# Attention stage of a hybrid decoder block: each projection in two halves of k, with one score unit and one head's maxima behind each half

## What is computed

```python
z = h @ w_in
q_b = apply_rope(aqkv[:, :, 0], cos, sin)
k_b = apply_rope(aqkv[:, :, 1], cos, sin)
for g, (window, dilation) in enumerate(((128, 1), (512, 4), (2048, 16))):
    s = jnp.where(valid, q @ k.T * 64 ** -0.5, -jnp.inf)   # blockwise, in the order of the dilation
    m = jnp.max(s, axis=-1)
    p = jnp.exp(s - m[..., None])
    l = jnp.sum(p, axis=-1)
    o = p @ v
wts = jnp.exp(ms - jnp.max(ms, axis=0))
o_b = (sum(wts * o) / sum(wts * l)) * silu(ag)
```

## Time and profile before

| | us |
|---|---|
| median of 3 runs | 1558.94 |
| lowest, highest | 1557.24, 1559.28 |
| profiled execution, its own time | 1559.48 |
| its span | 1557.7 |
| PE busy | 1536.4 |
| DVE busy | 835.1 |
| ACT busy | 671.9 |

### The profile page before, as it was taken

How to read it: one execution, slowest core, us unless ns; L and a number is a source line. 1 busy time by engine, 2 the same in 40 slices (tenths; PEclk the granted TensorE clock), 3 DMA queues, 4 the chain that set the end, 5 groups by cost and what they waited for, 6 DMA issues and landing times.

```text
span 1557.7 us, 21170 instructions
## 1 busy us (share of the span) xinstructions
PE 1536.4 (99%) x8088; PEld 1298.3 (83%) x8088; DVE 835.1 (54%) x1372; ACT 671.9 (43%) x842; POOL 46.8 (3%) x40
## 2 busy tenths in 40 slices
PE   7999999999999999999999999999999999999998
PEld 6888888888888888888888888888888888788987
DVE  6646565564636463767832574257435654643523
ACT  6646565555656474634323324332423235311211
POOL 2000000000000000002000000000000000000000
PEclk9999999999999999999999999999999999999999
DMA  5121211111111112122312121222122223232611
GB/s 213 42 68 55 68 47 47 54 67 54 67 54 54 54 54 67 54 81 68 95 42 55 55 69 56 56 55 60 50 56 67 55 89 109 95 128 96 243 42 81
DMA packets 33892, 113.73 MB, mean 73 GB/s; under 512 B 5338, under 2 KB 5788, under 8 KB 33820
## 3 DMA queue, kind: packets, MB, share of 16 engines
q1 hardware_dynamic: 33828, 112.82, 22.5%
HBM read 81.77 MB, written 18.45 MB: 64 GB/s over the span
## 4 chain that ended last, share of the span: by engine, by line
PE 97%; DVE 1%; DMA 1%; ACT 0%; SPq 0%; issue 0%
PE z_ps L629 21%; PE z_ps L627 21%; PE z_ps L628 21%; PE pc L792 4%; PE pb L654 3%; PE z_ps L857 2%; PE z_ps L859 2%; PE z_ps L858 2%; PE pa L738 1%; PE pb L775 1%; PE pb L760 1%; PE pb L771 1%; PE pb L768 1%; PE pc L691 1%; PE pb L646 1%; PE pa L859 1%
## 5 line engine op out<-in xcount | busy, mean ns | idle before, releaser
L627 PE MATMUL z_ps<-h_hi,w_hi 128*128 128x512 f32 x1392 | 557.2, 400 | 0.0
L629 PE MATMUL z_ps<-h_hi,w_lo 128*128 128x512 f32 x1392 | 549.5, 395 | 0.0
L628 PE MATMUL z_ps<-h_lo,w_hi 128*128 128x512 f32 x1392 | 549.1, 394 | 0.0
L629 PEld LDWEIGHTS z_ps<-h_hi,w_lo 128*128 128x128 f32 x1392 | 261.8, 188 | 61.4
L627 PEld LDWEIGHTS z_ps<-h_hi,w_hi 128*128 128x128 f32 x1392 | 262.3, 188 | 56.8 <-issue 0.4
L628 PEld LDWEIGHTS z_ps<-h_lo,w_hi 128*128 128x128 f32 x1392 | 262.3, 188 | 56.4
L1216 DVE TENSOR_TENSOR w_lo<-w_stage,w_hi 128x1024 fp32r<-128x1024 f32 x89 | 110.1, 1237 | 260.0 <-ACT w_hi L957 259.6
L965 ACT ACTIVATE zz<-z_ps 128x512 f32<-128x512 f32 x48 | 28.7, 598 | 213.4 <-PE z_ps L629 139.1
L965 ACT ACT_TABLE_LOAD x61 | 78.3, 1283 | 77.4 <-PE z_ps L629 76.7
L957 ACT ACTIVATE w_hi<-w_stage 128x1024 fp32r<-128x1024 f32 x89 | 93.8, 1054 | 0.4
L792 PE MATMUL pc<-pt,vb 128*128 128x128 f32 x560 | 76.9, 278 | 0.7 <-ACT pt L1123 0.7
(11 more groups left out here) (250 smaller groups left out, 2257.3 us busy)
## 6 DMA issues: line engine op xcount, KB each, us to landing
w_stage<-w_in SPq DMA_DIRECT2D x88, 512.0 KB, 3.5
z_swap<-zz SPq DMA_DIRECT2D x96, 128.0 KB, 2.3
gate_d<-gate SPq DMA_DIRECT2D x16, 512.0 KB, 3.7
x_in<-x SPq DMA_DIRECT2D x8, 512.0 KB, 7.4
o_a_d<-o_a SPq DMA_DIRECT2D x8, 512.0 KB, 4.7
w_stage<-w_a SPq DMA_DIRECT2D x8, 512.0 KB, 3.3
cos_t<-gate_d SPq DMA_DIRECT2D x8, 512.0 KB, 3.3
sin_t<-gate_d SPq DMA_DIRECT2D x8, 512.0 KB, 4.0
```

The lines of the kernel that those rows point to most:

```text
L627: nc.tensor.matmul(z_ps[hf][:], w_hi[s][:, k, :], h_hi[:, k, t], start=k == 0, stop=False)
L628: nc.tensor.matmul(z_ps[hf][:], w_hi[s][:, k, :], h_lo[:, k, t], start=False, stop=False)
L629: last = nc.tensor.matmul(z_ps[hf][:], w_lo[s][:, k, :], h_hi[:, k, t], start=False, stop=k == KT - 1)
```

## The change

PE's projection of a slot is cut in two: the first four steps of k (`front`), and the last four (`back`), into the same PSUM bank. Where there are units or maxima, all units of the slot but the last and the maxima of the first half of the list (head 0; in slot 16 the first pair (g, m)) stand between front and back; the last unit and the other maxima stand behind back. ACT's exponentials of the units that went between the halves now stand before the `take` of the slot. Nothing is added or removed, and DVE, POOL and SP have the program they had. Iteration 4 is as before.

```diff
--- before.py
+++ after.py
@@ -617,17 +617,21 @@
                         x_transpose(KT * hf + k + 4)
                 last.then_inc(z_made[hf], 1)
 
-            def project(n, s, hf):
-
-                if hf == 0:
-                    pe.wait_ge(w_lo_done, n + 1)
-                pe.wait_ge(z_taken[hf], n)
+            front, back = range(0, KT // 2), range(KT // 2, KT)
+
+            def project(n, s, hf, ks=range(KT)):
+
+                if ks[0] == 0:
+                    if hf == 0:
+                        pe.wait_ge(w_lo_done, n + 1)
+                    pe.wait_ge(z_taken[hf], n)
                 t = slice(HALF * hf, HALF * (hf + 1))
-                for k in range(KT):
+                for k in ks:
                     nc.tensor.matmul(z_ps[hf][:], w_hi[s][:, k, :], h_hi[:, k, t], start=k == 0, stop=False)
                     nc.tensor.matmul(z_ps[hf][:], w_hi[s][:, k, :], h_lo[:, k, t], start=False, stop=False)
                     last = nc.tensor.matmul(z_ps[hf][:], w_lo[s][:, k, :], h_hi[:, k, t], start=False, stop=k == KT - 1)
-                last.then_inc(z_made[hf], 1)
+                if ks[-1] == KT - 1:
+                    last.then_inc(z_made[hf], 1)
 
             def level_product(i, j):
 
@@ -796,17 +800,28 @@
             def attention(i, prev, cur):
                 for slot in range(2 * AT_CHUNKS):
                     c = slot // 2
+                    units = UNIT_SLOTS.get(slot, ()) if prev else ()
+                    peaks = [(g, m, h) for g, m in MAX_SLOTS.get(slot, ()) for h in range(2)] if cur else []
+
+                    def unit(u):
+                        scores_t(i, u)
+                        if u:
+                            weighted(i, u - 1)
+
                     if cur:
-                        project(N_HG + i * AT_CHUNKS + c, c % 2, slot % 2)
+                        project(N_HG + i * AT_CHUNKS + c, c % 2, slot % 2, front)
+                        for u in units[:-1]:
+                            unit(u)
+                        for g, m, h in peaks[:len(peaks) // 2]:
+                            maxima(i, g, m, h)
+                        project(N_HG + i * AT_CHUNKS + c, c % 2, slot % 2, back)
                     if first(i):
                         hgrn_tail(HEADS, slot)
                         if slot == 6:
                             pe.wait_ge(on_done, HEADS)
                     if prev:
-                        for u in UNIT_SLOTS.get(slot, ()):
-                            scores_t(i, u)
-                            if u:
-                                weighted(i, u - 1)
+                        for u in units[-1:] if cur else units:
+                            unit(u)
                         if slot == 11:
                             weighted(i, N_UNITS - 1)
                     if not cur:
@@ -818,10 +833,8 @@
                                 branch(0, 0, hf, (4, 5, 6, 7))
                             elif slot == 13:
                                 branch(0, 1, hf, (0, 1, 2))
-                    if cur:
-                        for g, m in MAX_SLOTS.get(slot, ()):
-                            for h in range(2):
-                                maxima(i, g, m, h)
+                    for g, m, h in peaks[len(peaks) // 2:]:
+                        maxima(i, g, m, h)
                     if cur and slot == 17:
                         maxed, summed = value(pe, i * N_MAX + N_MAX), value(pe, i * N_SUMS)
                         pe.wait_ge(const_in, 32)
@@ -1084,7 +1097,18 @@
                         for b in range(2):
                             dst = vb[:, g, 4 * b:4 * b + 4, :].rearrange("p c (x e) -> p c x e", e=EDIM)[:, :, 0:3:2, :]
                             nc.scalar.activation(dst, pb[:, b, :].rearrange("p (c x e) -> p c x e", c=4, x=2), ACT.Copy).then_inc(av_taken, 1)
+                    units = UNIT_SLOTS.get(slot, ()) if prev else ()
+
+                    def weigh(u):
+                        act.wait_ge(st_made, (i - 1) * N_UNITS + u + 1)
+                        cols = sum(P * k for _, _, k in unit_keys(UNITS[u][0], UNITS[u][2]))
+                        if u >= 2:
+                            act.wait_ge(pu_made, (i - 1) * N_UNITS + u - 1)
+                        nc.scalar.activation(pt[u % 2][:, 0:cols], pb[:, u % 2, 0:cols], ACT.Exp).then_inc(pt_done, 1)
+
                     if cur:
+                        for u in units[:-1]:
+                            weigh(u)
                         if c < 6:
                             if not first(i) or c >= 2:
                                 act.wait_ge(rope_sum, i * 6 + c - 1)
@@ -1114,13 +1138,8 @@
                         nc.scalar.activation(r_den[EDIM:P, :], acc[1][0:EDIM, :], ACT.Ln).then_inc(den_ln, 1)
                         act.wait_ge(den_ln, 2 * i)
                         nc.scalar.activation(r_den[:], r_den[:], ACT.Exp, scale=-1.0).then_inc(den_done, 1)
-                    if prev:
-                        for u in UNIT_SLOTS.get(slot, ()):
-                            act.wait_ge(st_made, (i - 1) * N_UNITS + u + 1)
-                            cols = sum(P * k for _, _, k in unit_keys(UNITS[u][0], UNITS[u][2]))
-                            if u >= 2:
-                                act.wait_ge(pu_made, (i - 1) * N_UNITS + u - 1)
-                            nc.scalar.activation(pt[u % 2][:, 0:cols], pb[:, u % 2, 0:cols], ACT.Exp).then_inc(pt_done, 1)
+                    for u in units[-1:] if cur else units:
+                        weigh(u)
                     if not cur:
 
                         if 1 <= slot < N_BR:
```

## The result

The changed kernel takes 1562.56 us, the median of 8 runs (1561.04 to 1563.59); the kernel before, in 8 runs beside it, 1558.79 (1557.24 to 1560.36). The ratio is 1.0026, 95% interval 1.0016 to 1.0035: a small slowdown, 3.8 us, clear of the noise. The profiled execution takes 1563.13 us, its span is 1561.4 us.

The account below looks back on a forecast made before the run. PE, busy throughout the attention stage, was taken as the bound. Boundaries 0.7, iteration 0's waits 1.74 and slot 15's 1.6 sum to 4.1 us, against the median 1558.94 giving 1563.0; range 1559.3 to 1566.5.

Parts of the forecast that it names:

- What bounds the kernel: Attention stage: PE busy 601.74 of 601.74 us, so no PE wait is left for the change to take away.
- rival of hidden waits: Weighted matmuls, slots 3 to 10 of iterations 1 to 3: hidden 0.1 us waits go, -4.1 us, 1554.8; chance 0.03.
- Part 1, boundaries: Projection cuts, iterations 0 to 3: 54 more excursions at 0.013 us each, 0.7 us in all.
- Part 2, exponentials: ACT's exponentials ahead of the take cost nothing; without cover each of the 27 slots with a front unit would pay.
- Part 3, iteration 0: PE waits for DVE's row maxima in slots 9, 11 and 13: 0.86, 0.18 and 0.70 us, delay 1.74.
- rival of absorbed waits: Iteration 0: DVE's work moves ahead, waits absent or absorbed; +0.7 to +2.3 us, about 1560.4; chance 0.29.
- Part 3, slot 15: Slot 15, four iterations: PE waits 0.41 us each for row maxima, whose release comes 0.24 later; 1.6 us.
- Slot 13 of iterations 1 to 3: Row maxima released at 1082.33, asked for at 1082.45: just passes without a wait, margin 0.12 us.
- The lengths of the iterations: Profile after: iteration 0 longer by about 2.3 to 2.4 us, iterations 1 to 3 by about 0.6 each.
- The lock: Iteration 0: DVE's chain slips with PE, so waits add up, +4.3 for 1.74; +6.7, 1565.6; chance 0.06.
- The clock: PE's granted clock falls behind the new waits, all seven adding 10 us: 1566 to 1573; chance 0.04.

Follow-up runs that it names:

- maxima undivided: Changed kernel with both heads' maxima behind the back half again, cut and units between the halves kept; ratio to before 0.9997.
- 24 further ones: Changed kernel with 24 more excursions out of the projection in slots 3 to 10 of iterations 1 to 3; ratio to before 1.0020.
- later cut: Changed kernel with its projection cut behind step 6 of 8 instead of 4; ratio to before 0.9999.
- short product: Changed kernel with DVE's product of z_swap and the sines done for 64 of 1024 columns in iteration 0; ratio to before 1.0005.
- second bank: Changed kernel with the maxima of slots 9, 11 and 13 of iteration 0 written to PSUM pair pb; ratio to before 1.0006.
- undivided slot 13: Changed kernel, but in slot 13 alone both heads' maxima stand behind the whole projection; ratio to before 1.0011.
- cut behind step 2: Changed kernel with its projection cut behind step 2 instead of 4; 1574.57 us against 1559.38 before, ratio 1.0097.
- exponentials behind the take: Changed kernel with ACT's exponentials of the front units back behind the take in slots 3 to 10; 1571.31 us, ratio to before 1.0079.

## Why the prediction was right

Its number was 1563.0; measured is 1562.56, and +3.8 against the forecast +4.1. The stage, which is what the sum describes, lost 3.3; that the medians stand nearer to the forecast than the stage does is chance within their noise (the interval is 2.5 to 5.5 us). The stage makes up the 3.3 from 1.66 in slots 9, 11 and 13, 1.25 in the four slots 15 and 0.4 elsewhere; the prediction had 1.74, 1.64 and 0.7. By its own steps:

- **What bounds the kernel.** Right: PE had no wait that the change could take away. The rival of hidden waits would have shown shorter slots with units; slots 3 to 10 of iteration 1 are 0.01 to 0.03 longer. With all maxima undivided, the units between the halves gave back nothing.
- **Part 1, boundaries.** Predicted 0.7 us, 0.013 for each of 54. Measured, beside slot 15, iterations 1 to 3 lost 0.12 to 0.17 each, 0.44 in 45 excursions, 0.01 each; 24 further ones took nothing. The range (0 to 0.02) held. The Trainium skill ("TensorE: Matmul & The Clock Gate", Part 2, "Step-by-step") has only an isolated matmul pay its drain; by that page's warm formula 54 excursions isolated twice would be an estimated 18 us, near 1577. No run shows a boundary that isolates a matmul.
- **Part 2, exponentials.** Right that they cost nothing in the new order, and that, for one, slot 3 pays 0.64 us without it. The cover is less even than the text had it: the shortfall without the edit falls on 18 slots, not on every slot with a front unit.
- **Part 3, iteration 0.** Slot 9: 0.86 predicted, 0.80 measured. Slot 11: 0.18 and 0.21. Slot 13: 0.70 and 0.65. The later cut, the short product and the second bank each take these away by another road: asked later, released sooner, not needed. The rival of absorbed waits needed DVE to gain 0.86 us by slot 9; it gained 0.02.
- **Part 3, slot 15.** 0.41 predicted each time; 0.29 to 0.32 measured. The path was right, as the undivided slot 13 shows, but two terms were mis-sized. The request was put 2.79 us behind the slot's start, half of what slot 9's projection takes. Slot 15 starts behind transposes, and there the first step takes 0.31 us instead of 0.23. The kernel before, iteration 2, the second and the thirteenth matmul of slot 15 (the first is in the earlier trace rows):

```profile
1092.85 0.39 PE L628 MATMUL z_ps<-h_lo,w_hi 128*128 128x512 f32 x1
...
1095.40 0.40 PE L627 MATMUL z_ps<-h_hi,w_hi 128*128 128x512 f32 x1
```

The half is 1095.40 - 1092.54 = 2.86 us there, so PE asks 0.07 later than the sum has it. The other term is the lag: put at 0.20, it is 0.06 from DVE's end to PE's start and 0.10 of slower restart, 0.16. With both the sum gives 0.41 - 0.07 - 0.04 = 0.30.
- **Slot 13 of iterations 1 to 3** just passed, as said (6.03 or 6.04 us against 6.05 or 6.06 before).
- **The lengths of the iterations** grew by less than forecast, for the same terms: iteration 0 by 1.95 us instead of 2.3 to 2.4, iterations 1 to 3 by 0.44 to 0.47 each instead of about 0.6.
- **The lock** did not come: slots 10 and 12 took 6.05 and 6.06 (6.07 and 6.03 before), and the cut behind step 2 made iteration 0 longer by 5.1 and not 9. **The clock** did not fall in the stage, with waits of up to 0.7 us and, with the earlier cut, sixteen shown waits of up to 1.5: the granted clock is 1.00 over the stage in both.

## What to carry to other kernels

Where an engine is never idle, as PE in this stage, moving its own work ahead has no wait to remove, but it asks for its inputs earlier. So list for each moved instruction when its release comes, and which engine sets it. Count how late that release is against the schedule of before: each earlier wait has already made the request later and covers a part of it. Measure the distance from a slot's start to the request in the very slot, since not every half projection takes the same. And see what stands behind the moved work: here the projection's end came later by one head's maxima, and a chain over ACT and DVE charged that to PE two slots further on.

## What was not expected of the hardware

PE has one longer wait that has nothing to do with the change, near 1360 us: it waits for DVE, and DVE for a load of the gates. What the clock does behind it differs from run to run. The changed kernel, PE's waiting instruction and the window behind it; then the kernel with slot 13 undivided:

```profile
1362.90 0.47 PE L870 MATMUL z_ps<-h_hi,w_hi 128*128 128x512 f32 x1 [2.03 <-DVE part L1602]
...
1363.30:1366.30 3.00, 3.00 (x9) 2.35 (x8) 1.50 (x4) 0.00 (x0) 0.00 (x0) 0.50 0.42 168
```

```profile
1360.81 0.47 PE L870 MATMUL z_ps<-h_hi,w_hi 128*128 128x512 f32 x1 [2.30 <-DVE part L1602]
...
1360.80:1363.80 3.00, 2.99 (x13) 2.47 (x14) 1.77 (x4) 0.00 (x0) 0.00 (x0) 1.00 0.53 214
```

After 2.03 us of waiting the clock stood at 0.50, 1.2 GHz, for the next 3 us; after 2.30 us in the other it stayed at 1.00. Of eleven profiles six have the fall (before, changed, maxima undivided, both other cuts, exponentials behind the take) with 278.2 to 278.5 us from the last slot of iteration 3 to the end, and five don't, with 276.3 to 277.1. The length of the wait does not sort them: 1.97 to 2.31 us in the six, 1.78 to 2.30 in the five. The mean granted clock of the whole run does: 0.998 in the six, 0.999 or 1.000 in the five. By the same mark 27 runs of the kernel before fall apart without overlap: 22 at 0.998 took 1559.05 to 1560.89 us, 5 at 0.999 took 1557.66 to 1558.21. So in one program it comes and goes between executions; that it is the same fall in the runs without a trace is inferred from the mark. The step between the medians of the two groups is 1.4 us, more than a third of what was measured here. It can turn a comparison around: with all maxima undivided the median is 0.9 us under the kernel before, yet among runs with the same mean clock it is 1.0 and 0.3 us over it, as the 0.5 us of the stage say. For effects of this size it is the length of the stage in the trace that tells, not the total.
